# A state space layer's second group: decays spread over six units, heads and gating two units later

## What is computed

```python
zxbcdt = x @ w_in                       # z, x, B, C of all groups, and dt
xbc = silu(conv4(xbc))                  # 4-tap causal convolution per feature
dt = softplus(dt_raw + dt_bias); da_cum = cumsum(dt * a)
decay_in = exp(_segsum(da))             # exp of differences of cumulative sums
y_diag = einsum(cb, decay_in, x_c)      # cb = C B^T
y = y_diag + y_off + xs * d_skip        # y_off: what the first chunk gives the second
y = y * silu(z)                         # the gating
y = y * rsqrt(mean(y*y per group) + eps) * norm_w
h = y @ w_out
```

## Time and profile before

| | us |
|---|---|
| median of 3 runs | 2111.7 |
| lowest, highest | 2110.71, 2111.87 |
| the profiled execution, its own time | 2109.32 |
| span of that profile | 2107.5 |
| PE busy in it | 2096.1 (99%) |
| DVE busy, ACT busy | 1539.2 (73%), 1135.2 (54%) |
| mean granted TensorE clock | 0.998 of full |

### The profile page before, as it was taken

How to read it: one execution, slowest core, us unless ns; L and a number is a source line. 1 busy time by engine, 2 the same in 40 slices (tenths; PEclk the granted TensorE clock), 3 DMA queues, 4 the chain that set the end, 5 groups by cost and what they waited for, 6 DMA issues and landing times.

```text
span 2107.5 us, 27512 instructions
## 1 busy us (share of the span) xinstructions
PE 2096.1 (99%) x10886; PEld 1771.5 (84%) x10886; DVE 1539.2 (73%) x2040; ACT 1135.2 (54%) x1411; POOL 52.3 (2%) x42
## 2 busy tenths in 40 slices
PE   9999999999999999999999999999999999999999
PEld 7878888888888888888888888888888888888887
DVE  7788788778777877675675556556778687787775
ACT  6766565565664556563555445545445455445452
POOL 0000000000000000000010011000000000000000
PEclk9999999999999999999999999999999999999999
DMA  8555565554554654445465545455576666666663
GB/s 326 199 210 191 200 210 180 208 209 170 204 190 179 211 173 161 140 158 198 179 221 172 200 169 173 160 186 209 185 239 195 219 208 199 221 188 208 240 180 140
DMA packets 68144, 411.28 MB, mean 195 GB/s; under 512 B 7472, under 2 KB 14384, under 8 KB 20656
## 3 DMA queue, kind: packets, MB, share of 16 engines
q1 hardware_dynamic: 66000, 394.85, 52.5%
q0 software_dynamic: 2016, 14.68, 3.8%
HBM read 407.27 MB, written 2.23 MB: 194 GB/s over the span
## 4 chain that ended last, share of the span: by engine, by line
PE 93%; DVE 1%; ACT 0%; POOL 0%; issue 0%; DVEq 0%
PE bank L1087 24%; PE bank L1108 15%; PE bank L1112 15%; PE bank L1110 15%; PE bank L1091 12%; PE bank L1124 2%; PE bank L1126 2%; PE bank L1128 2%; PE bank L1204 1%; PE bank L1342 1%; PE bank L1278 1%; PE bank L1300 0%; PE bank L1237 0%; PE bank L1330 0%; PE bank L1355 0%; PE bank L1311 0%
## 5 line engine op out<-in xcount | busy, mean ns | idle before, releaser
L1838 DVE TENSOR_TENSOR wlo<-raw,whi 128x2048 fp32r<-128x2048 f32 x318 | 727.8, 2289 | 250.1 <-ACT whi L1406 216.3
L1406 ACT ACTIVATE whi<-raw 128x2048 fp32r<-128x2048 f32 x318 | 608.4, 1913 | 287.0 <-PE bank L1112 272.2
L1087 PE MATMUL bank<-A,whi 128*128 128x512 f32 x2448 | 587.7, 392 | 0.0
L1087 PEld LDWEIGHTS bank<-A,whi 128*128 128x128 f32 x2448 | 451.1, 188 | 91.7 <-issue 2.2
L1091 PEld LDWEIGHTS bank<-A,wlo 128*128 128x128 f32 x2448 | 313.9, 191 | 11.9
L1108 PE MATMUL bank<-whi,A2h 128*128 128x512 f32 x800 | 314.6, 393 | 3.4 <-DVE W L1906 3.4
L1091 PE MATMUL bank<-A,wlo 128*128 128x256 f32 x2448 | 317.4, 283 | 0.0
L1110 PE MATMUL bank<-whi,A2l 128*128 128x512 f32 x800 | 312.3, 390 | 0.0
L1112 PE MATMUL bank<-wlo,A2h 128*128 128x512 f32 x800 | 312.0, 390 | 0.0
L1108 PE MATMUL bank<-whi,A 128*128 128x512 f32 x608 | 241.8, 398 | 0.0
L1112 PE MATMUL bank<-wlo,A 128*128 128x512 f32 x608 | 237.8, 391 | 0.2
(11 more groups left out here) (262 smaller groups left out, 1828.7 us busy)
## 6 DMA issues: line engine op xcount, KB each, us to landing
raw<-wst SPq DMA_DIRECT2D x313, 1024.0 KB, 4.8
W<-wst SPq DMA_DIRECT2D x33, 1024.0 KB, 5.5
W<-wst POOLq DMA_DIRECT2D x9, 1024.0 KB, 8.0
W<-cum_scratch SPq DMA_DIRECT2D x8, 1024.0 KB, 7.2
W<-rows SPq DMA_DIRECT2D x21, 256.0 KB, 5.8
raw<-wst POOLq DMA_DIRECT2D x5, 1024.0 KB, 8.2
raw<-wst SPq DMA_DIRECT2D x16, 256.0 KB, 7.0
W<-exp_scratch SPq DMA_DIRECT2D x16, 256.0 KB, 6.2
```

What stands on the lines that cost most here:

```text
L1087: e.matmul(o[:, :], whi[:, s, k * P:(k + 1) * P], A1[:, k, :, :].rearrange("p h t -> p (h t)"), start=k == 0, stop=False)
L1406: e.activation(whi[:, u % 3, :], raw_of(u), ACT.Copy).then_inc(*hi.inc((u, 3)))
L1838: e.tensor_tensor(wlo[:, u % 3, :], raw_of(u), whi[:, u % 3, :], ALU.subtract).then_inc(*lo.inc((u, 3)))
```

## The change

Only the steps of group 1 are moved. The differences are made one head at a time at n = 6, 7, 8 and 9, then two at n = 10 and two at n = 11. The two Exp and their mask products move from n = 8 and 9 to n = 9 and 11, the skip terms from n = 8 to n = 11, `heads_out` from n = 10 and 11 to n = 12 and 13, and all that follows (gating, squares, high and low parts, row means, rsqrt) by two units, as does SP's load of the cumulative sums of group 2. SP's load of group 1's exponentials stays at n = 10. The order of ACT's semaphore marks is adapted. Groups 0 and 2 to 7 have the order they had: `LATE` gives them 2 and 0, `DECAYS` the steps 8, 9 and 7, 8. No instruction is added to or taken from the list; where Exp and Silu now alternate, the compiler places further ACT_TABLE_LOAD instructions.

```diff
+LATE = (2, 4) + (0,) * (NG - 2)
+DECAYS = ((8, 9), (9, 11)) + ((7, 8),) * (NG - 2)
...
-            run(("ssd", g), start, 17 if g == 1 else 15)
+            run(("ssd", g), start, 15 + LATE[g])
...
         def ssd_act(g):
             names = [f"d{half}{h}" for h in range(HG) for half in "AB"]
-            names[12 if g == 0 else 16:0] = ["e0"]
-            if g:
-                names.append("e1")
-            names[13 if g == 0 else 17 if g == 1 else 18:0] = words("k0 k1 k2 k3")
+            k = words("k0 k1 k2 k3")
             if g == 0:
-                names.append("e1")
+                names = (*names[:12], "e0", *k, *names[12:], "e1")
+            elif g == 1:
+                names = (*names[:8], "e0", *names[8:], "e1", *k)
+            else:
+                names = (*names, "e0", "e1", *k)
...
-                late = 2 if g < 2 else 0
+                late = LATE[g]
...
             if g == 1:
-                return {6: (0, 1, 2), 7: (3, 4, 5), 8: (6, 7)}.get(n, ())
+                return {6: (0,), 7: (1,), 8: (2,), 9: (3,), 10: (4, 5), 11: (6, 7)}.get(n, ())
...
-                if n in (7 + late // 2, 8 + late // 2):
-                    decays(g, n - 7 - late // 2)
-                if n == 8:
+                if n in DECAYS[g]:
+                    decays(g, DECAYS[g].index(n))
+                if n == (11 if g == 1 else 8):
                     w.wait_ge(s_co, 16)
...
-                if n in (7 + late // 2, 8 + late // 2):
-                    hh = n - 7 - late // 2
+                if n in DECAYS[g]:
+                    hh = DECAYS[g].index(n)
...
-                if n == 14 + (2 if g < 2 else 0):
+                if n == 14 + LATE[g]:
```

## The result

The changed kernel takes 2106.0 us (median of 10 executions, 2104.06 to 2107.09) where the kernel before takes 2111.29 (10 executions beside them: nine from 2110.3 to 2112.5, whose own median is 2111.22, and one of 2976.64). By the medians the change gains 5.3 us, the size that was forecast (2106.4 for 2111.7). The profiled execution took 2105.25 us, with a mean clock of 1.000 of full for 0.998. Lines of the changed kernel are those of before plus 5.

A forecast was written before the change was run, and what follows sets the result against it. TensorE, busy 2096.1 of 2107.5 us, was taken as the bound. An earlier unit 21 (3.57 us) plus a held clock (1.75) make 5.3 us, so 2106.4 for a median of 2111.7; range 2105.0 to 2109.4.

The forecast's parts named there:

- The term of the clock: At unit 21: the clock stays at full, so the unit takes 5.55 us instead of 7.30, a gain of 1.75 us.
- Steps 1 to 4: Ahead of unit 21: fewer heads (1.39 us), mask product m0 (1.75) and a 0.42 wait gone; it starts 3.57 us earlier.
- Step 3: On DVE ahead of unit 21: m0 leaves, ACT's copies are done by 130.3, the first add starts at 133.67 for 137.24.
- Step 5: Ahead of unit 21: the DVE chain lo(21), a0, a1, `tl` (4.85 us) is late next; about 1.7 us of pause stay.
- Step 6: Pause ahead of unit 21 shrinks from 5.55 to 1.98 us and the clock holds, 1.75 us gained; two in three.
- rival A: At unit 21 the clock falls all the same: gain only 3.8 us, time 2107.9; chance 0.25.
- Where the moved work lands: Units 21 to 28 and on: ACT and DVE have room, the moved work is hidden; 3.2 us to spare at unit 30.
- rival C: Units 25 to 28: the moved work makes DVE the bound and TensorE stalls at unit 30; slower, 2116; chance 0.06.
- The table loads: On ACT, group 1's e1 and the next Silu need a load each, 2 x 1.28 = 2.6 us, hidden.
- B: At unit 21: something else held the add, so the unit starts where it did; no gain, 2111.7; 0.09 together with D.
- D: On ACT: too many table switches make hi(25) over 5.6 us late, unit 25 stalls; 2109 at worst; 0.09 together with B.

## Why the prediction was right, step by step

The places of the gain were right, and the number was right in part by luck. The start of unit 21 moved by 3.59 us for 3.57. The term of the clock was 1.75 us, and in the two profiles compared it is 1.77, but the medians are made otherwise, as "The number" below tells.

Distances from lo(20) to unit 21, and what the steps said:

| kernel | distance, us | less than before | forecast |
|---|---|---|---|
| before | 14.27 | | |
| changed | 10.68 | 3.59 | 3.57 |
| heads alone | 12.87 | 1.40 | 1.39 |
| decays and skip terms late | 12.07 | 2.20 | 2.18 |
| heads_out and gating late | 14.25 | 0.02 | 0 |
| skip terms back | 12.87 | 1.40 | |

- **Steps 1 to 4 (heads 1.39, m0 and the wait 2.18, together 3.57)** hold to 0.02 us, the heads and the rest each by an experiment of its own. Step 3 took for granted that ACT's copies come in time since the skip terms go; the kernel with the skip terms back shows that the whole 2.18 hangs on it.
- **Absolute times** were wrong by a microsecond: unit 21 at 135.17 for 134.15, hi(21) at 127.86 for 126.8, gating at 165.22 for about 162, `tl` of group 1 at 179.30 for 178. "I am wrong if unit 21 starts after 135" was thus met although the mechanism held. An execution's own shift, 1.04 us of DVE's chain here, passes straight into such a time; the criterion should have been a distance. Gating is off by more, since sum and gating stand behind lo(27), which waited 1.32 us for hi(27) and ends at 163.3, a wait that I had not counted; it had room.
- **Step 5 (the pause shrinks to 1.98 us; the next is the DVE chain)**: the pause from 132.58, the end of unit 20, to 135.17 is 2.59 us; the difference is what is left when DVE's chain is 1.04 us later and TensorE only 0.41. That this chain is next was shown by taking the adds out of it (0.83 us more).
- **Step 6 (the clock holds, 1.75 us, two in three)**: where it holds, unit 21 takes 5.53 us. By the mean clock it held in six of ten executions, near the two in three; where the four others lost it no trace tells, and of the two later executions with such a mean one lost it at this place (1.6 us), one at the kernel's start. "It holds or it falls" was the wrong form: both happen. The reason given for holding, that unit 21 restarts ahead of the point at which the clock fell in the profile of before (2.2 us behind unit 20), was not borne out. That point is not fixed: it lay 2.2, 2.3, 2.6, 4.4 and 4.6 us behind unit 20 in the five profiles with pauses of 3.7 us and more and nothing put into them. And the changed kernel's clock held where unit 21 restarted 2.59 us behind unit 20 and fell where it restarted 1.94 us behind. The 3 us at half rate of rival A stood in no row of before; 3.4 were measured.
- **The number.** By the six executions at 1.000 (2105.06) and the nine ordinary ones of before (2111.22) a held clock gains 6.2 us, by the kernel with two constant matmuls 6.0, where the forecast says 5.3 for it. The likely reason, seen in single profiles and not shown for the medians: the fall in the old pause cost 1.75 us in the profile of before, but up to 2.8 us in the other profiles with a pause of over 4 us, and that profile, at 2109.32, is some 2 us under the median of its kernel. The forecast took these 2 us (2.4 by its three executions) for an offset that the change leaves alone. That error is made good in the median of 2106.0 by the four executions at 0.999, so the agreement within 0.4 us is in part luck.
- **Where the moved work lands: nothing.** From the start of unit 25 to the end of the span it is 1942.9 us before, 1943.0 in the changed kernel and 1943.0 in the kernel in which only heads_out and gating moved. From unit 21 to unit 25 it is 25.13 in the changed kernel and 25.33 in the kernel before with 12 constant matmuls, both at full clock. And lo(30) ends at 185.5 and unit 30 starts at 189.35, 3.8 us to spare for 3.2 forecast. DVE is busy for 5.42 of 5.56 us in unit 28 (the window 177.11 to 182.67), so it is near its limit, as rival C had it, but never ahead of TensorE's need. SP's cumulative sums go out at 154.71; nobody waits for them.
- **The table loads.** The second Exp comes behind a load, and the next Silu too. From group 1's first Exp to that Silu there are four loads where there were two; three of them:

```profile
138.64 1.28 ACT L1468 ACT_TABLE_LOAD   x1
145.67 1.28 ACT L1564 ACT_TABLE_LOAD   x1
146.96 1.49 ACT L1564 ACTIVATE W<-W 128x1536 f32<-128x1536 f32 x1
148.36 1.69 ACT L1550 ACTIVATE W<-W,CO 128x256 f32<-128x256 f32 x4
...
168.38 1.28 ACT L1465 ACT_TABLE_LOAD   x1
```

Exp stands 1.29 us behind its load, as in the earlier trace rows: the two instructions that the change adds to ACT (1413 for 1411) cost 2.6 us of it and no time. The Trainium skill's rule (ScalarE: Activation LUTs, "Rules for kernel authors") against switching between table sets speaks of ACT's own time; here ACT had it. The page's 2.66 us for a switch were not seen.

- **The rivals.** B (no gain) and D (switches) fall with the distance of 10.68 and with a wait list that holds nothing new; C (DVE the bound in units 25 to 28) with the 3.8 us at unit 30. A (3.8 us, 2107.9) is true of at least one execution, in its mechanism and in its size up to unit 25 (3.7 us), the fall costing 1.6 us where I had 1.5. Its time of 2107.9 does not fit (2106.21 there), most likely for the reason under "The number", and it does not hold for the median.

What stays open: what sets the phase of ACT and DVE ahead of unit 20 in an execution (lo(20) starts between 123.45 and 125.46 us over all profiles), and what decides whether the clock falls at a pause, and at which point of it. The length of the pause alone does not: in three profiles of the changed kernel it held over 1.34 and 2.59 us and fell behind 1.94. What a typical execution of the kernel before loses to the clock is open too, as it has one profile only.

## What to carry to other kernels

When TensorE waits on another engine's chain, count the chain's pieces back to the last point at which that chain itself waited; each piece taken out is worth its own duration, until a second chain of equal end is met, and here both (mask product on DVE, skip terms on ACT) had to leave together. Do not take the price of a clock fall from one profile. Check a forecast by the distance from an event ahead of the change, never by a time from the span's start. Small work that stood in the pause cost its full length; the same work inside the run of output units cost nothing.

## What the runs showed of the hardware

- A delay of TensorE of 1.43 us ahead of the pause did not reach unit 21: it came 0.20 us later, by which DVE's lo(20) was later too (10.68 us from one to the other in both).
- The clock fell to 1.2 GHz 0.6 to 1.3 us after work had started again at full clock, behind pauses of 1.94 us (135.6, restart 134.49) and 3.74 us (137.3, restart 136.62) and, at the start of a kernel, behind a wait of 1.46 us (11.5, restart 10.25); or in the pause itself where that was 4.2 to 5.6 us long, between 2.2 and 4.6 us behind the end of unit 20. In the kernel before with 6 constant matmuls in the pause it fell at 135.7, while those ran.
- It stayed low for some 3.4 us in four profiles and for some 6.8 in four others. From unit 21 to unit 25 the fall cost 1.6 us where all of 3.4 low us lay over matmuls that count, and 1.75 to 2.8 where 6.8 low us lay partly in the pause.
- With two or five constant matmuls in the changed kernel's pause the mean clock was 1.000 in 19 of 19 executions, without them in six of twelve, the two single ones counted.
- An fp32 matmul of 128x256 on constants was recorded as two, of some 0.22 us each (24 for 12, 10 for 5), which made my fillers twice as long as planned.
